# Seven slots of split weights and more seven-product steps in a two-block float32 kernel

## What is computed

```python
u = jnp.square(jax.nn.relu(jnp.einsum('bsd,df->bsf', h, w_ff1[l])))      # first block, D_FF = 8192
x = x + jnp.einsum('bsf,fd->bsd', u, w_ff2[l])
...
gate, val = jnp.split(y, 2, axis=-1)                                     # second block, D_FF_2 = 5632
return (jax.nn.silu(gate) * val) @ w_down
```

## Time and profile before

| | |
|---|---|
| median of three runs | 2383.93 us (2383.45 to 2384.9) |
| the profiled execution | 2383.46 us, span 2381.6 us |
| PE busy | 2376.9 us, 100% of the span, 12581 matmuls |
| PE weight loads | 2035.4 us, 85% (they overlap the matmuls) |
| DVE busy | 1700.7 us, 71% |
| ACT busy | 1216.5 us, 51% |
| DMA | 190 GB/s, queue of the weights 59.3% of 16 engines |
| granted TensorE clock | 1.0 over the span |

### The profile page before, as it was taken

How to read it: one execution, slowest core, us unless ns; L and a number is a source line. 1 busy time by engine, 2 the same in 40 slices (tenths; PEclk the granted TensorE clock), 3 DMA queues, 4 the chain that set the end, 5 groups by cost and what they waited for, 6 DMA issues and landing times.

```text
span 2381.6 us, 30785 instructions
## 1 busy us (share of the span) xinstructions
PE 2376.9 (100%) x12581; PEld 2035.4 (85%) x12581; DVE 1700.7 (71%) x1804; ACT 1216.5 (51%) x1427; POOL 0.2 (0%) x4
## 2 busy tenths in 40 slices
PE   9999999999999999999999999999999999999999
PEld 8888888888888888888888888888888888888887
DVE  6565666666568868868768667855778778886788
ACT  5444454554545445445445555555555455545554
POOL 0000000000000000000000000000000000000000
PEclk9999999999999999999999999999999999999999
DMA  7566556666555665655665565555655665566655
GB/s 253 160 187 196 167 185 196 191 188 196 186 187 178 219 216 189 213 181 198 202 190 193 182 185 160 171 183 186 186 181 194 196 192 176 186 219 186 188 173 181
DMA packets 238040, 452.15 MB, mean 190 GB/s; under 512 B 16569, under 2 KB 20779, under 8 KB 237771
## 3 DMA queue, kind: packets, MB, share of 16 engines
q1 hardware_dynamic: 237147, 449.07, 59.3%
q10 hardware_dynamic: 752, 1.12, 0.1%
HBM read 446.46 MB, written 3.67 MB: 189 GB/s over the span
## 4 chain that ended last, share of the span: by engine, by line
PE 97%; DVE 2%; ACT 0%; issue 0%; ACTq 0%; DVEq 0%
PE PS L684 41%; PE PS L686 21%; PE PS L717 11%; PE PS L718 11%; PE PS L719 11%; DVE WL L1279 1%; PE PS L648 0%; PE PS L615 0%; PE PS L636 0%; PE PS L657 0%; ACT WH L840 0%; PE PS L542 0%; PE PS L625 0%; DVE PB L1259 0%; PE PS L553 0%
## 5 line engine op out<-in xcount | busy, mean ns | idle before, releaser
L1279 DVE TENSOR_TENSOR WL<-RAW,WH 128x1024 fp32r<-128x1024 f32 (+1 forms) x844 | 1002.0, 1204 | 520.6 <-ACT WH L840 519.1
L684 PE MATMUL PS<-XHL,WH 128*128 128x512 f32 x3968 | 1248.9, 396 | 0.0
L840 ACT ACTIVATE WH<-RAW 128x1024 fp32r<-128x1024 f32 (+1 forms) x845 | 867.5, 1041 | 744.4 <-PE PS L686 478.3
L686 PEld LDWEIGHTS PS<-XHL,WL 128*128 128x128 f32 x3968 | 745.4, 188 | 176.0
L686 PE MATMUL PS<-XHL,WL 128*128 128x256 f32 x3968 | 779.7, 278 | 0.0
L684 PEld LDWEIGHTS PS<-XHL,WH 128*128 128x128 f32 x3968 | 605.1, 189 | 2.1 <-issue 1.0
L717 PE MATMUL PS<-WH,MHL 128*128 128x512 f32 x1000 | 390.2, 390 | 0.0
L719 PE MATMUL PS<-WH,MHL 128*128 128x512 f32 x1000 | 389.2, 389 | 0.0
L718 PE MATMUL PS<-WL,MHL 128*128 128x512 f32 x1000 | 389.1, 389 | 0.0
L719 PEld LDWEIGHTS PS<-WH,MHL 128*128 128x128 f32 x1000 | 187.7, 188 | 39.3
L717 PEld LDWEIGHTS PS<-WH,MHL 128*128 128x128 f32 x1000 | 187.7, 188 | 38.8 <-issue 0.3
(11 more groups left out here) (212 smaller groups left out, 1374.6 us busy)
## 6 DMA issues: line engine op xcount, KB each, us to landing
RAW<-in_w_ff SPq DMA_DIRECT2D x256, 512.0 KB, 4.1
RAW<-in_w_in SPq DMA_DIRECT2D x224, 512.0 KB, 3.9
RAW<-in_w_up SPq DMA_DIRECT2D x176, 512.0 KB, 4.1
RAW<-in_w_down SPq DMA_DIRECT2D x88, 512.0 KB, 4.4
RAW<-in_w_mix_out SPq DMA_DIRECT2D x32, 512.0 KB, 4.0
RAW<-in_w_out SPq DMA_DIRECT2D x32, 512.0 KB, 3.7
RAW<-in_w_conv_out SPq DMA_DIRECT2D x16, 512.0 KB, 3.7
RAW<-in_w_attn_out SPq DMA_DIRECT2D x16, 512.0 KB, 4.3
```

Of the source, the lines that this page charges most:

```text
L684: mm(PS[:, b + p.banks[j], :], h[:, k, j * P:(j + 1) * P], x[:, kc, :], start=st, stop=False)
L686: t = mm(PS[:, b + p.banks[j], 0:T], l[:, k, j * P:(j + 1) * P], x[:, kc, 0:T], start=False, stop=en)
L840: act(high, raw, AF.Copy).then_inc(*own.made(hi, i))
L1279: tt(low, raw, high.bitcast(f32), sub).then_inc(*own.made(lo, i))
```

## The change

The slots become seven in the feed-forwards: two more, `WHX` and `WLX`, lie in memory that attention and convolution use at other times. They join the rotation at the first entry of the first `ff` item and leave it ahead of the item `("ff2", 3, 2)`; they join again at the first `gate` item of the second block. `ahead_of(n, most)` goes as far ahead as slots allow: the split of entry m waits for the entry that had its slot, `prior[m]`, and is called at the first n beyond it, which is n + 4 with five slots and n + 6 with seven. `SEVEN` is (2, 4, 6) of eight pairs in both feed-forwards and (2, 4) of six. The activation sums `AXH` and `AXL` get a third place, `AS` moves into the unused end of `PB`, and the loads of the final gain (`GF`) and of the attention bias (`BIAS`) move to a later place in the SP queue, as does the addition of the mask to `BIAS` on DVE. The functions `group`, `sevens` and `take` are as before.

```diff
+NX = 2
-SEVEN = {"ff": (2, 4), "down8": (4, 5), "down6": (3,)}
+SEVEN = {"ff": (2, 4, 6), "down8": (2, 4, 6), "down6": (2, 4)}
...
-            AXH = sb("AXH", [P, 2, 4, P], f32r, c=c)
-            AXL = sb("AXL", [P, 2, 4, P], f32r, c=c)
-            AS = sb("AS", [P, 4, P], c=c)
+            AXH = sb("AXH", [P, 3, 4, P], f32r, c=c)
+            AXL = sb("AXL", [P, 3, 4, P], f32r, c=c)
...
+            WHX = sb("WHX", [P, NX, UNIT], f32r, c=c)
+            WLX = sb("WLX", [P, NX, UNIT], f32r, c=c)
...
+        more = {item_of["ff", 0, 0].parts[0].ent: branches_end, item_of["gate", 0].parts[0].ent: item_of["wo", 0].end}
+        fewer = (item_of["ff2", 3, 2].parts[0].ent,)
+        turns, slot, prior = [(n, None) for n in range(NS)], [], []
+        for n in range(len(ents)):
+            if n in more:
+                turns = [(NS + i, more[n]) for i in range(NX)] + turns
+            if n in fewer:
+                turns = [t for t in turns if t[0] < NS]
+            place, before = turns.pop(0)
+            slot.append(place)
+            prior.append(before)
+            turns.append((place, n))
+        more_used = max(n for n in range(fewer[0]) if slot[n] >= NS)
+
+        def ahead_of(n, most):
+
+            last = n
+            while last + 1 < len(ents) and last < n + most and (prior[last + 1] is None or prior[last + 1] < n):
+                last += 1
+            return last
...
-        BIAS_AFTER = ents[item_of["ff", 1, 0].parts[0].ent][1] + AHEAD - 1 + NR
-        branches_end = item_of["attn", 3].end
+        x_end = item_of["ff", 3, 3].end
+
+        GF_AFTER, BIAS_AFTER = (ents[n + NS + NX + 1][1] + NR for n in (x_end, more_used))
...
-                    if i >= NS:
-                        own.wait_ge(*used[i - NS])
+                    if prior[i] is not None:
+                        own.wait_ge(*used[prior[i]])
                     act(high, raw, AF.Copy).then_inc(*own.made(hi, i))
...
                         for ent in st.ents:
                             split_to(ent)
-                            split_to(ent + AHEAD)
+                            split_to(ahead_of(ent, NS + NX))
                             work.pump()
                             if not st.seven:
                                 work.pump()
...
-                elif it.key == ("ff", 3, 1):
+                elif it.key == ("K", 0):
                     chain()
                     own.wait_ge(s_wp, 16)
                     tt(BIAS[:], BIAS[:], over4(M, 8), add).then_inc(*own.made())
```

More of the change, by code:

```diff
@@ L107 @@
     mid: dict = field(default_factory=dict)
-    ahead: int = AHEAD
+    ahead: int = NS + NX
     n: int = 512
@@ L202, in first_half @@
             self.put("proj", ("q", half), self.wide(w1, 0, ALLK, C0["q"] + 512 * half), ("X", "mix"), args=h,
-                     mid=mid if half == 0 else {}, ahead=1 if half == 0 else AHEAD)
+                     mid=mid if half == 0 else {}, ahead=1 if half == 0 else NS + NX)
             self.put("proj", ("k", half), self.wide(w1, 0, ALLK, C0["k"] + 512 * half), ("X", "mix"), args=h,
@@ L308, in build @@
         XT = sb("XT", [P, 2, D])
+        with ExitStack() as c:
+            sb("Xpad", [P, 12 * 2 * T], c=c)
+            GF = sb("GF", [P, D], c=c)
         XHL = sb("XHL", [P, NKC, 2 * T], f32r)
@@ L406, in build, with high_slot, low_slot @@
         units, ents, items = plan.units, plan.ents, plan.items
+        item_of = {it.key: it for it in items}
+        branches_end = item_of["attn", 3].end
+        more = {item_of["ff", 0, 0].parts[0].ent: branches_end, item_of["gate", 0].parts[0].ent: item_of["wo", 0].end}
[16 more added lines that the diff above has]
+            return last
+        def high_slot(n):
+            return WH[:, slot[n]] if slot[n] < NS else WHX[:, slot[n] - NS]
+        def low_slot(n):
+            return WL[:, slot[n]] if slot[n] < NS else WLX[:, slot[n] - NS]
         def landed(u):
@@ L413, in raw_view, with wviews @@
             return RAW[:, u % NR, 0:per * n].rearrange("p (k n) -> p k n", k=per)
-        def wview(buf, e):
+        def wviews(e):
             what, u = ents[e]
             _, per, n = units[u] if what != "b22" else (None, 1, 512)
-            return buf[:, e % NS, 0:per * n].rearrange("p (k n) -> p k n", k=per)
+            return [b[:, 0:per * n].rearrange("p (k n) -> p k n", k=per) for b in (high_slot(e), low_slot(e))]
         def paired(e):
-            return WH[:, e % NS, 0:NKC * 16].rearrange("p (k n) -> p k n", k=NKC)
+            return high_slot(e)[:, 0:NKC * 16].rearrange("p (k n) -> p k n", k=NKC)
         def pieces(e):
@@ L426, in pieces @@
             n = units[u][1] * units[u][2]
-            raw, high, low = RAW[:, u % NR, 0:n], WH[:, e % NS, 0:n], WL[:, e % NS, 0:n]
+            raw, high, low = RAW[:, u % NR, 0:n], high_slot(e)[:, 0:n], low_slot(e)[:, 0:n]
             if units[u][2] == 8:
@@ L513, in sync @@
                     del waiting[:3]
+                if i == GF_AFTER:
+                    own.wait_ge(*used[x_end])
+                    e.dma_start(GF[:], io["g_final"].rearrange("(a n) -> a n", a=1).to_broadcast([P, D])
+                                ).then_inc(s_gf, 16)
                 if i == BIAS_AFTER:
                     own.wait_ge(s_er, er_all)
-                    own.wait_ge(*used[branches_end])
+                    own.wait_ge(*used[more_used])
                     e.dma_start(BIAS[:], bass.AP(ERD.tensor, ERD.offset + P - 1, [[8 * 384 - 1, P], [384, 8], [1, T]])
                                 ).then_inc(s_wp, 16)
-                    e.dma_start(GF[:], io["g_final"].rearrange("(a n) -> a n", a=1).to_broadcast([P, D])
-                                ).then_inc(s_gf, 16)
             for g in range(2):
@@ L1171, in parts @@
                     split_to(p.ent)
-                    split_to(p.ent + it.ahead)
+                    split_to(ahead_of(p.ent, it.ahead))
                     work.pump()
@@ L1215, in scalar @@
                     split_to(it.end)
-                    split_to(it.end + AHEAD)
+                    split_to(ahead_of(it.end, AHEAD))
                 elif it.steps:
```

14 lines of the change are left out of this document (6 added, 8 removed).

## The result

The changed kernel takes 2501.18 us (median of four, 2496.02 to 2502.85), against 2384.41 of the kernel before: a ratio of 1.0485, with a 95% interval of 1.0471 to 1.0498. It is slower by 117 us; forecast was 2457, slower by 73, with a range up to 2476. The profiled execution took 2502.85 us, its span is 2501.1 us, 119.5 more than before.

What follows compares the result with a forecast made beforehand. The prediction took PE's sequence of matmuls to bound the kernel. From 2383.46 us: - 8.8 (saved matmuls) + 22.2 (short holes) + 45.6 (long holes) + 2.8 (tail) + 12 (clock) = 2457 us, range 2431 to 2476.

Steps and rivals of the forecast that it cites:

- The cover: Behind each group's last seven-product step: one plain pair, 5.44 us, follows in all 13 groups, against a release at 9.12 us.
- Short holes, 3.7 us: PE idle where a plain item follows a group: 9.12 us release less 5.44 cover, six times, 22.2 us.
- Long holes, 7.6 us: PE idle where a second group follows: release 13.0 us behind the step less 5.44, six times, 45.6 us.
- The landing: Ahead of a second group, sums13 waits for a raw unit going into entry 22's buffer: 4.1 us.
- The backlog: DVE's queued work from the group's start, 35.0 us, finishes entry 22 1.0 us ahead of the last step's end.
- The clock, 12 us: PE's slow clock behind holes: 2.0 us behind each 7.6 us hole, 0 behind those of 3.7.
- Rival 2: PE's clock is lost behind every hole, 2.5 us each, 12 x 2.5 instead of 12; 2475 us, chance 0.09.
- Rival 1: The same holes without any clock loss behind them; 2445 us, chance 0.32.
- Mask addition at nothing, at most 2.4: Mask added onto BIAS on DVE, moved into an item with plain entries: costs nothing, at most 2.4 us.
- The tail, 2.8 us: Behind the very last group: the last output addition ends 3.7 us behind PE, before 0.96; cost 2.8 us.
- rival 4: DVE falls behind inside the groups as well, half the added steps showing 2.2 us; 2471 us, chance 0.09.
- Rival 3: Banks come free within the plain pair, so no holes; 2374.6 us, decided at a 6.2 us release, chance 0.05.

## Why the prediction was right in kind and wrong in size

**Savings.** 39 matmuls of 512 columns, 8.8 us: the count is exact. Right.

**The cover.** That one plain pair of 5.44 us follows the last step, that line 1640 is what PE then waits for, and that 12 holes come of it, all was as the prediction had it. The run with 24 late steps shows that position alone does it, the run with two plain pairs that cover removes it.

**Short holes, 3.7 us.** Five are 3.58 to 3.64. Right. The sixth, behind the first block's last group, is 6.8: wrong by 3.1. ACT waited 1.5 and 2.5 us for weights ahead of its copy there, so late landings are the likely cause, but no run took them away.

**Long holes, 7.6 us, between 6.3 and 8.3.** They are 9.3 to 12.4, 63.9 us instead of 45.6. The ledger has three terms, and DVE's timeline has each of them. From the start of sums13 to the release it had 9.95 us; all six holes have 9.8. The two other terms are the steps that failed:

- The landing, a single wait of 4.1 us between entry 22 and sums13. It is 5.2, 5.6 and 6.3 us in the first block and 6.5, 5.8 and 5.9 in the second, 10.6 us more in all, because the loads are issued in a burst at DVE's pace.
- The backlog, entry 22 done 1.0 us ahead of the end of the step. It is done 0.2, 0.2 and 0.4 us ahead in the first block and 1.6, 1.1 and 1.0 us behind in the second, 9.0 us more in all.

The first long hole of the second block has the most of both. The step ended at 1920.07 - 12.38 - 0.17 - 5.44 = 1902.1, and the first of these four low parts, which is the ledger's entry 22, at 1903.7:

```profile
1902.51 4.81 DVE L1316 TENSOR_TENSOR WL<-RAW,WH 128x1024 fp32r<-128x1024 f32 x4
1910.19 1.23 DVE L1296 TENSOR_TENSOR PB<-RAW 128x1024 f32<-128x1024 f32 x1 [2.87 <-DMA RAW<-in_w_down]
```

With half the weights the wait is 3.4 us in four of the six holes, 3.9 and 4.4 in the others, and the backlog is what it was. So the 7.5 to 7.8 us of the first block in that run meet the 7.6 of the ledger by luck: the wait is shorter than 4.1 and the backlog larger, and the two cancel. The second block's holes stay 1.2 to 2.7 us above it by the backlog. Why DVE is later there was only argued: the ledger was made for the first block's evacuation and took the second's, with its eight tap operations, as equal.

**The clock, 12 us.** The step that failed is "0 for those of 3.7". The granted clock is 0.50 behind short holes too. The balance of the span, 119.5 + 8.8 - 88.7 - 2.0 (slot ends) - 4.0 (the two other waits) - 2.8 (tail), leaves 30.8 us for it. The starts of the 40 matmuls behind each hole agree: the twelve stretches lost 29.6 us, 1.6 to 2.9 each, and the one behind line 615 1.7. Filling the holes gave 25.5 back. Rival 2 of the prediction had this term nearly right, at 30 us. Rival 1 leaned on a granted clock that never moves in the trace of before. At the start that reading doesn't fit the matmuls: they took 0.236 us where they later take 0.111, half the pace.

**Mask addition at nothing, at most 2.4.** 2.2 us of wait and, with the clock behind it, 3.9 in the run that isolates the slots. The step that failed is that nothing would wait for it. I named the cost and did not look at who waits behind it: DVE's first piece of an evacuation, on which PE's next small products wait.

**The tail, 2.8 us.** Behind PE's last slot the span goes on for 6.3 us, 3.5 before: 2.8. Right.

**The other rivals.** DVE falling behind inside the groups (rival 4) cost 1.8 us with seven slots. The sentence "more lead can't make PE wait" was wrong with the new steps, and the ledger of the long holes, which has the next group's sums ahead of the evacuation because of that lead, spoke against it: with five slots these holes are 4.8 to 6.5 us, with seven 9.3 to 12.4. Rival 3, the release in time, did not come up by itself; with the evacuation ahead of the splits the release stood at 6.8 us where that rival had reckoned 6.3, and it decides at 6.2.

The terms add up: 18.3 (long holes) + 3.1 (the hole behind the first block's last group) - 0.5 (the five short holes) + 18.8 (clock) + 2.2 (mask, wait) + 1.8 (low parts) + 2.0 (slot ends) is 45.7 us, and from 2457.3 to the profiled 2502.9 it is 45.6.

## What to carry to other kernels

When work is moved later, ask what used to lie between it and the next claim on the same banks: here three matmuls saved per step were paid with the plain pairs that had hidden 9 us of evacuation. A price read where events come evenly (4.1 us for a landing) doesn't hold where a late engine releases them in a burst. And a pause of PE should be priced with the slow clock that may stand behind it, here 1.5 to 2.9 us, nearly as much as the shorter pauses themselves. The length of the pause alone did not tell: 1.9 us was followed by it in one place, 3.6 us in another was not.

## What the runs showed of the hardware

I had not expected the clock to fall behind pauses as short as 3.6 us. Granted clock 0.50 (1.2 GHz) stood behind holes of 9.3 us and, for part of the stretch, of 3.6 and of 1.9 us; the starts of 512-column matmuls are 0.43 us apart there and 0.227 at 2.4 GHz. Behind the 1.3 us holes of the run with evacuation first the granted clock reads 1.00 and the matmuls went at full pace, and so they did behind one hole of 3.6 us in the run with 24 late steps. The wait of 2.2 us at line 615 was followed by a clock of 0.66 in the run with the steps where they were, and by 1.00 in the one with evacuation first and two plain pairs. The Trainium skill ("TensorE: Matmul & The Clock Gate", section "What's actually happening") has idleness throttle the array to half its clock; these traces agree, with 5.71 us for 13 starts that take 2.95 at full clock.
